# Reordering the input stage of a two-layer decoder kernel: x ahead of the tables, two bias products in two column groups

## The chip, the cores and the metric

The kernel runs on one NeuronCore of one Trainium2 chip, in one launch. The metric is the device time of that core in microseconds (us). Before the change the median of three runs is 1153.02 us (1152.75 to 1153.35). Engines are named as the profile names them: PE (TensorE), PEld (its weight loads), DVE (VectorE), ACT (ScalarE), POOL (GpSimd), SP (SyncE); SPq and ACTq are the issuing of DMAs on SP and on ACT.

## The reference: what is computed

A decoder trunk of two layers on x of 512 tokens by 1024 channels, all in float32. Layer 0 has sparse attention with an indexer that picks 128 keys per query, layer 1 sliding-window attention with sinks; each is followed by a SwiGLU block.

```python
for layer in range(DEPTH):
    h = rms_norm(x, attn_norm[layer])
    if layer % N_MIXERS == 0:
        x = x + dsa_mixer(h, a_w_in[j], a_latent_norm[j], a_w_uv[j], a_w_out[j], rel_bias)
    else:
        x = x + swa_mixer(h, b_w_in[j], b_b_in[j], b_sinks[j], b_w_out[j], b_b_out[j], rel_bias)
    h = rms_norm(x, ffn_norm[layer])
    x = x + swiglu(h, ffn_w_gate_up[layer], ffn_w_down[layer])
return rms_norm(x, final_norm)
```

Both mixers add a bias to their logits, `rel_bias[rel_bucket(distance)]`, from one table of 32 buckets by 16 heads. The part of the kernel that the change touches is what stands ahead of the first projection `h @ a_w_in`: x has to be loaded and turned so that channels lie on partitions, the norm gains have to be turned, and the bias table is spread out over distances.

## The kernel before

The order of the work is written out by hand, one program for each engine, with semaphores between them. x is held turned, as eight blocks (m = 0 to 7) of 128 channels by 512 tokens. Nearly all matrix products are done three times over in a rounded type (`mm3`, lines 613 to 615): high weights by high x, high weights by low x, low weights by high x. Weights come from memory as slabs of 128 x 2048 in `raw`. For each half of a slab (128 x 1024) ACT writes the rounded part `w_hi` (line 1162), then POOL writes the rest `w_lo` (line 501), then PE may use it (`lo_done`).

The input stage, which is the first 15 us or so, goes as follows.

- SP issues, in this order, the identity `tab` (L401), the 59 rows of norm gains and biases `par_rows` (L402), the first half of the channels of x for token blocks 0 and 2 (L395), half of the first weights (L399), the second half of x for these blocks, the rest of the first weights, the masks `tab_a` (L408) and the second slab (L410). It then waits for `g_sb` and stores it as `bias_row` (L414). Of `x_tok`, each DMA moves 128 tokens by 512 channels, 256 KB.
- ACT issues the one-hot table `hot` (33 rows of 4 KB, L1198), `rel_sb` (the bias table, L1199), and both halves of x for token blocks 1 and 3 (L1203). "fore" is the first half of the channels (all four DMAs add to the semaphore `x_in_fore`), "rear" the second.
- PE turns `par_rows` (L677), and multiplies `rel_sb` by the two halves of `hot` in two products of 512 columns (L681 into bank 6 and L684 into bank 7, both on output partitions 0 to 15, the second behind a wait for `par_done`). Then it turns x with 32 transposes of 128 x 128 (L671), 16 for the fore half and 16 for the rear half. Then it begins the first projection (L613 to L615).
- DVE copies the turned gains to `params` (L1603), the two products to `g_sb` (L1608, L1609), and for each block of x it makes `xs_lo` (L1614) and the copy `x` (L1618).
- ACT makes `xs_hi` for each block (L1211). Behind blocks 1 and 5 it casts a half of the first weights slab (L1162); POOL follows with `w_lo` (L501).

The first projection product waits for `lo_done` of the first half slab, for `xlo_done` of block 0, and for two blocks of `x`. Being in order on PE, it also stands behind all 32 transposes.

Of the kernel before, what the change touches and what calls it, by code (L numbers as in the profile page):

```python
# [7 lines left out]
F32 = mybir.dt.float32  # L8
# [6 lines left out]
T = 512  # L15
# [4 lines left out]
H = 16  # L20
# [4 lines left out]
BUCKETS, MAX_DIST = 32, 128  # L25
# [15 lines left out]
C_ID, C_DUP, C_CAUSAL, C_HOT = 0, P, 2 * P, 3 * P  # L41
ROW_A, ROW_B = 640, 384
GLEN = ROW_A + ROW_B
C_END = C_HOT + GLEN

S_A1, S_A2, S_AO, S_F0, S_D0 = 0, 3, 11, 15, 37
S_BK, S_BQ, S_BO, S_F1, S_D1, S_END = 53, 54, 58, 62, 84, 100
# [30 lines left out]
def tables():  # L78

    t = np.zeros((P, C_END), np.float32)  # L80
    i = np.arange(P)
# [13 lines left out]
def trunk(nc, x_in, rel_bias, par_in, a_w_in, a_w_uv, a_w_out, b_w_in, b_sinks, b_w_out,  # L95
          w_gate_up, w_down, consts, bias_row, bias_toep, out):
    ctx = ExitStack()
    with ctx:
        def sb(name, shape, dt=F32, where=ctx):
            return where.enter_context(nc.sbuf_tensor(name, shape, dt))  # L100

        def sem(name):
            return ctx.enter_context(nc.semaphore(name))
# [44 lines left out]
        early = ExitStack()  # L148
        x_tok = sb("x_tok", [P, NB, D], F32, early)
        hot = sb("hot", [BUCKETS + 1, GLEN], F32, early)  # L150
        g_sb = sb("g_sb", [H, GLEN], F32, early)
        rel_sb = sb("rel_sb", [BUCKETS + 1, H], F32, early)
        par_rows = sb("par_rows", [59, P], F32, early)
        early.close()
# [77 lines left out]
        ps = ctx.enter_context(nc.psum_tensor("ps", [P, 8, T], F32))  # L232
# [16 lines left out]
        hot_in = sem("hot_in")  # L249
# [10 lines left out]
        g_mm, g_done, row_out, toep_out = sem("g_mm"), sem("g_done"), sem("row_out"), sem("toep_out")  # L260
# [58 lines left out]
        def _(sp):  # L319
            def slab(n, it, src):  # L320

                for dst, s in src(n % 2):
                    if n == S_BK + 2:

                        sp.wait_ge(lo_done, 2 * (S_BK - 1))
                    elif n >= 2:

                        sp.wait_ge(lo_done, 2 * (n - 1) + 4 * it)
                    sp.dma_start(dst, s).then_inc(raw_full[n % 2], 16)

            def wide(w, c0):

                def src(slot):
                    v = raw[:, slot, :].rearrange("p (k n) -> p k n", k=DM)
                    g = w.rearrange("(k p) n -> p k n", p=P)
                    return [(v[:, 4 * i:4 * i + 4, :], g[:, 4 * i:4 * i + 4, bass.ds(c0, 256)])
                            for i in range(2)]
                return src
# [52 lines left out]
            def x_part(half):  # L391

                c = slice(half * T, (half + 1) * T)
                for t in (0, 2):
                    sp.dma_start(x_tok[:, t, c], x_in[0, t * P:(t + 1) * P, c]).then_inc(x_in_s[half], 16)  # L395

            def latent_part(k, n, done):

                sp.dma_start(r0[:, k:k + n, :], aw[:, k:k + n, A_CKV:A_CKV + 2 * P]).then_inc(done, 16)  # L399

            sp.dma_start(tab[:, 0:P], consts[:, 0:P]).then_inc(id_in, 16)  # L401
            sp.dma_start(par_rows[:, :], par_in).then_inc(small_in, 16)  # L402
            x_part(0)
            latent_part(0, 4, raw_fore)
            x_part(1)
            for k in (4, 6):
# [4 lines left out]
                    .then_inc(raw_full[1], 16)  # L411

            sp.wait_ge(g_done, 2)
            sp.dma_start(bias_row, g_sb[:, :]).then_inc(row_out, 16)  # L414
            slab(2, 0, wide(a_w_in[0], A_QI + P))
            sp.dma_start(sink[:, :], b_sinks[0:1, :].broadcast_to([P, H])).then_inc(sink_in, 16)
            sp.dma_start(uv_raw[:, :, :], a_w_uv[0].rearrange("h r c -> r h c")).then_inc(uv_full, 16)
            sp.wait_ge(row_out, 16)
            for n in range(S_A2, S_AO):
                slab(n, 0, wide(a_w_in[0], (n - S_A2) * 256))  # L420
                if n < S_A2 + 4:
# [75 lines left out]
        def _(pool):  # L497
# [29 lines left out]
            def q_part(h):  # L527

                if h == 0:

                    pool.wait_ge(row_out, 16)

                pool.wait_ge(qh_done, h + 1)
                nc.gpsimd.tensor_tensor(q_lo[:, h, :], q_new[h % 2], q_hi[:, h, :].bitcast(F32),
                                        ALU.subtract).then_inc(ql_done, 1)

            split_lo(S_A2 + 2)
            for h in range(3):
                q_part(h)
# [6 lines left out]
            for h in range(3, 7):  # L546
                q_part(h)
            for i in range(3, 6):
                split_lo(S_A2 + 2 + i)
                q_part(2 * i + 1)  # L550
                q_part(2 * i + 2)
# [58 lines left out]
        def _(pe):  # L610
# [52 lines left out]
            def x_turn(half):  # L663

                pe.wait_ge(x_in_s[half], 16 * NB)
                for m in range(half * DM // 2, (half + 1) * DM // 2):
                    if m == 6:

                        pe.wait_ge(g_done, 2)
                    for t in range(NB):  # L670
                        last = nc.tensor.transpose(ps[:, m, t * P:(t + 1) * P],  # L671
                                                   x_tok[:, t, m * P:(m + 1) * P], ident)
                    last.then_inc(x_tr, 1)
# [4 lines left out]
            pe.wait_ge(hot_in, 32)  # L678
            pe.wait_ge(rel_one, 1)

            nc.tensor.matmul(ps[0:H, 6, :], rel_sb[:, :], hot[:, 0:T], start=True, stop=True).then_inc(g_mm, 1)  # L681

            pe.wait_ge(par_done, 1)
            nc.tensor.matmul(ps[0:H, 7, 0:GLEN - T], rel_sb[:, :], hot[:, T:GLEN], start=True, stop=True).then_inc(g_mm, 1)  # L684
            x_turn(0)
            x_turn(1)

            pe.wait_ge(x_new, 2)
# [13 lines left out]
            for i in range(1, NB):  # L702
                last = nc.tensor.transpose(ps[:, 7, i * JI:(i + 1) * JI], kw[DH:DH + JI, i * P:(i + 1) * P],
                                           ident[DH:DH + JI, DH:DH + JI])
# [297 lines left out]
            for s in range(NB):  # L1002
                last = nc.tensor.transpose(ps[:, 7, s * P:(s + 1) * P], kv[:, 1, s * P:(s + 1) * P], ident)
# [139 lines left out]
        def _(act):  # L1143
# [41 lines left out]
            def xs_hi_m(m):  # L1185
                return xs_hi[:, bass.ds(m * T, T)]
# [8 lines left out]

                nc.scalar.activation(spare[:, 0:1], eps[:, :], func)

            act.dma_start(hot[:, :], consts[0:BUCKETS + 1, C_HOT:C_END]).then_inc(hot_in, 16)  # L1198
            act.dma_start(rel_sb[0:BUCKETS, :], rel_bias).then_inc(hot_in, 16)  # L1199
            for half in range(2):  # L1200
                c = slice(half * T, (half + 1) * T)
                for t in (1, 3):
                    act.dma_start(x_tok[:, t, c], x_in[0, t * P:(t + 1) * P, c]).then_inc(x_in_s[half], 16)  # L1203

            act.wait_ge(set_up, 4)
            load_table(ACT.Sqrt)
# [2 lines left out]
            for m in range(DM):  # L1209
                act.wait_ge(x_tr, m + 1)  # L1210
                nc.scalar.activation(xs_hi_m(m), ps[:, m, :], ACT.Copy,  # L1211
                                     scale=params[:, GAIN[0] + m:GAIN[0] + m + 1]).then_inc(xhi_done, 1)
                if m in (1, 5):
                    split_half(0, m // 4)
            split_hi(1)
            for m in range(DM):
# [351 lines left out]
        def _(dve):  # L1568
# [20 lines left out]
            def norm(e):  # L1589
# [14 lines left out]
            dve.wait_ge(par_done, 1)  # L1604
            nc.vector.tensor_scalar(nq_bias[:, :], params[:, B_IN:B_IN + DM], -float(DH) ** -0.5, None, ALU.mult)\
                .then_inc(nqb_done, 1)
            dve.wait_ge(g_mm, 2)
            nc.vector.tensor_copy(g_sb[:, 0:T], ps[0:H, 6, :]).then_inc(g_done, 1)  # L1608
            nc.vector.tensor_copy(g_sb[:, T:GLEN], ps[0:H, 7, 0:GLEN - T]).then_inc(g_done, 1)  # L1609

            for m in range(DM):

# [383 lines left out]
```

## Time and profile before

| | |
|---|---|
| median of 3 runs | 1153.02 us (1152.75 to 1153.35) |
| the profiled execution: its own time | 1152.82 us |
| its span, from first to last instruction | 1151.0 us |
| PE busy | 1135.0 us, 99% |
| DVE, ACT, POOL busy | 43%, 39%, 51% |
| PE first busy at | 5.38 us |
| first projection product (L613) starts at | 15.34 us |

The profile is of one execution, with times from the start of the span. A group of instructions is told as line, engine, operation, the tile written and the tiles read. Matmuls are pipelined, so that the duration of one is longer than the distance to the next: of 512 columns in the rounded type one takes 0.39 us and the next begins 0.23 us later. A float32 product shows as two instructions (x2). For a DMA the profile gives the time from issue to landing, where it could be found. The chain of waits is followed back from the last instruction.

### The profile page before, as it was taken

What the parts mean: (1) busy time and instruction counts of PE and PEld (TensorE: products, weight loads), DVE (VectorE), ACT (ScalarE), POOL (GpSimd) and SP (SyncE); (2) the same over time, 40 slices, a digit from 0 to 9 for tenths busy, and PEclk for the clock granted to TensorE, in tenths of its full rate; (3) what the DMA queues carried; (4) which work ended last, traced back from release to release, by engine and by line L of the source; (5) the groups of instructions that cost most, each with busy time, mean ns of one, the idle gap of its engine ahead of it and who ended that gap; (6) DMA issues with size and microseconds to landing.
All of it is one profiled execution on the core that took longest, in us unless ns stands there. A gap on an engine that the chain in (4) does not pass through costs nothing.

```text
span 1151.0 us, 15730 instructions
## 1 busy us (share of the span) xinstructions
PE 1135.0 (99%) x5538; PEld 928.1 (81%) x5538; DVE 496.7 (43%) x873; ACT 444.5 (39%) x829; POOL 590.7 (51%) x325
## 2 busy tenths in 40 slices
PE   8999999999999999999999999999999999999997
PEld 6778888778888888888888887788888888888887
DVE  6489956623534444441111366455443443420001
ACT  5353267743432322322222477544233233232333
POOL 4427767844544545434444487654454454444441
PEclk9999999999999999999999999999999999999999
DMA  7442311223233332324433333123323323223231
GB/s 240 160 138 73 129 37 56 74 74 109 75 109 89 93 109 80 102 80 123 147 111 108 98 98 78 38 84 99 110 73 109 102 81 109 84 78 98 79 100 73
DMA packets 180531, 112.45 MB, mean 98 GB/s; under 512 B 6300, under 2 KB 174551, under 8 KB 180488
## 3 DMA queue, kind: packets, MB, share of 16 engines
q1 hardware_dynamic: 179820, 110.71, 32.2%
q10 hardware_dynamic: 668, 1.19, 0.3%
q8 instruction: 24, 0.39, 0.1%
q14 instruction: 19, 0.16, 0.0%
HBM read 109.72 MB, written 8.45 MB: 103 GB/s over the span
## 4 chain that ended last, share of the span: by engine, by line
PE 93%; DVE 2%; POOL 2%; issue 1%; ACT 1%; DMA 0%; ACTq 0%; DVEq 0%; SPq 0%
PE ps L613 28%; PE ps L615 28%; PE ps L614 28%; PE ps L871 1%; PE ps L851 1%; DVE work L1691 1%; PE ps L622 1%; PE ps L1062 1%; POOL b_prob L596 1%; PE ps L822 1%; POOL w_lo L501 1%; PE ps L1036 1%; PE ps L671 1%; DVE work L1673 0%; DMA par_rows<-in_parameter_rows 0%
## 5 line engine op out<-in xcount | busy, mean ns | idle before, releaser
L501 POOL TENSOR_TENSOR w_lo<-raw,w_hi 128x1024 fp32r<-128x1024 f32 (+1 forms) x198 | 454.3, 2318 | 478.0 <-ACT w_hi L1162 469.6
L613 PE MATMUL ps<-xs_hi,w_hi 128*128 128x512 f32 x960 | 377.2, 393 | 1.1 <-DVE q_odd L1655 0.6
L614 PE MATMUL ps<-xs_lo,w_hi 128*128 128x512 f32 x960 | 373.7, 389 | 0.0
L615 PE MATMUL ps<-xs_hi,w_lo 128*128 128x512 f32 x960 | 373.6, 389 | 0.0
L1162 ACT CAST w_hi<-raw 128x1024 fp32r<-128x1024 f32 (+1 forms) x194 | 177.1, 963 | 434.8 <-PE ps L615 434.8
L613 PEld LDWEIGHTS ps<-xs_hi,w_hi 128*128 128x128 f32 x960 | 180.2, 188 | 41.9 <-issue 2.2
L614 PEld LDWEIGHTS ps<-xs_lo,w_hi 128*128 128x128 f32 x960 | 180.2, 188 | 37.7 <-issue 1.0
L615 PEld LDWEIGHTS ps<-xs_hi,w_lo 128*128 128x128 f32 x960 | 180.2, 188 | 37.8
L613 PE MATMUL ps<-act_hi,w_hi 128*128 128x512 f32 (+1 forms) x374 | 141.6, 378 | 0.0
L615 PE MATMUL ps<-act_hi,w_lo 128*128 128x512 f32 (+1 forms) x374 | 140.9, 377 | 0.0
L614 PE MATMUL ps<-act_lo,w_hi 128*128 128x512 f32 (+1 forms) x374 | 140.8, 377 | 0.0
L1813 DVE TENSOR_TENSOR glu<-std,up 128x512 f32<-128x512 f32 x44 | 67.8, 1540 | 77.0 <-ACT std L1365 76.8
L1816 DVE TENSOR_TENSOR act_lo<-glu,act_hi 128x512 f32 (+1 forms) x44 | 74.9, 1703 | 42.8 <-ACT act_hi L1370 42.8
L1809 DVE TENSOR_TENSOR up<-ps,rstd 128x512 f32<-128x512 f32 x44 | 30.4, 691 | 138.6 <-PE ps L615 138.6
L1828 DVE TENSOR_TENSOR x<-ps,x 128x512 f32 (+1 forms) x15 | 10.4, 692 | 173.7 <-PE ps L615 173.7
L614 PEld LDWEIGHTS ps<-act_lo,w_hi 128*128 128x128 f32 x374 | 70.4, 188 | 12.8
L615 PEld LDWEIGHTS ps<-act_hi,w_lo 128*128 128x128 f32 x374 | 70.4, 188 | 12.8
L613 PEld LDWEIGHTS ps<-act_hi,w_hi 128*128 128x128 f32 x374 | 70.4, 188 | 12.7
L1370 ACT CAST act_hi<-glu 128x512 f32 (+1 forms) x44 | 27.3, 622 | 76.9 <-DVE glu L1813 76.9
L596 POOL TENSOR_SCALAR b_prob<-b_prob,b_rinv 128x256 f32<-128x256 f32 x48 | 46.1, 977 | 11.8 <-DVE b_rinv L1885 11.8
L1578 DVE SCALAR_TENSOR_TENSOR xs_lo<-x,params,xs_hi (+1 forms) x24 | 25.5, 1063 | 51.6 <-ACT xs_hi L1177 51.6
L561 POOL TENSOR_SCALAR prob<-prob,rinv 128x512 f32<-128x512 f32 (+2 forms) x24 | 29.5, 1246 | 16.6 <-DVE rinv L1758 16.6
(186 smaller groups left out, 1255.6 us busy)
## 6 DMA issues: line engine op xcount, KB each, us to landing
raw<-in_ffn_w_gate_up SPq DMA_DIRECT2D x88, 512.0 KB, 4.5
raw<-in_ffn_w_down SPq DMA_DIRECT2D x32, 384.0 KB, 3.4
raw<-in_ffn_w_down SPq DMA_DIRECT2D x32, 320.0 KB, 3.9
raw<-in_a_w_in SPq DMA_DIRECT2D x19, 512.0 KB, 5.1
bias_toep<-bias_row SPq DMA_DIRECT2D x4, 1024.0 KB
toep<-bias_toep SPq DMA_DIRECT2D x16, 256.0 KB, 2.6
raw<-in_a_w_out SPq DMA_DIRECT2D x8, 512.0 KB, 4.3
raw<-in_b_w_in SPq DMA_DIRECT2D x8, 512.0 KB, 4.9
```

Source lines behind the costliest of these rows:

```text
L501: nc.gpsimd.tensor_tensor(pieces(w_lo, n)[half], pieces(raw, n)[half], pieces(w_hi, n)[half].bitcast(F32), ALU.subtract)\
L561: nc.gpsimd.tensor_scalar(at, at, rinv[:, par, i:i + 1], None, ALU.mult).then_inc(nrm_done, 1)
L596: nc.gpsimd.tensor_scalar(at, at, b_rinv[:, k % 3, a, i:i + 1], None, ALU.mult)\
L613: nc.tensor.matmul(dst, wh, xh, start=start, stop=False, **kw)
L614: nc.tensor.matmul(dst, wh, xl, start=False, stop=False, **kw)
L615: return nc.tensor.matmul(dst, wl, xh, start=False, stop=stop, **kw)
L1162: nc.scalar.copy(pieces(w_hi, n)[half], pieces(raw, n)[half]).then_inc(hi_done, 1)
L1370: nc.scalar.copy(act_hi[:, j + 2 * it, :], glu[:, j % 2, :]).then_inc(ah_done, 1)
L1578: nc.vector.scalar_tensor_tensor(xs_lo[:, bass.ds(m * T, T)], x[:, m, :], params[:, bass.ds(gain + m, 1)], xs_hi[:, bass.ds(m * T, T)].bit ...
L1809: nc.vector.tensor_tensor(up[:, :], ps[:, b + 1, :], rstd[:, :], ALU.mult).then_inc(up_done, 1)
L1813: nc.vector.tensor_tensor(glu[:, v, :], silu[:, :], up[:, :], ALU.mult).then_inc(glu_done, 1)
L1816: nc.vector.tensor_tensor(act_lo[:, v + 2 * it, :], glu[:, v, :], act_hi[:, v + 2 * it, :].bitcast(F32), ALU.subtract)\
```

## The change

Four edits, all in the input stage.

1. On SP, the fore half of x (blocks 0 and 2) is issued ahead of `tab` and `par_rows`.
2. On ACT, the fore half of x (blocks 1 and 3) is issued ahead of `hot` and `rel_sb`, the rear half behind them.
3. The two bias products write the same PSUM bank 6, the first on partitions 0 to 15, the second on partitions 32 to 47 (`G_REAR` = 32), one right behind the other without the wait for `par_done` between them, which moves behind the turning of the fore half. `g_sb` takes the same form, 48 partitions by 512. DVE waits once for both products, and `bias_row` is stored by two DMAs of 32 KB in place of one of 64 KB.
4. ACT casts the first half slab of weights behind the first block of x and no longer behind the second.

```diff
-        g_sb = sb("g_sb", [H, GLEN], F32, early)
+        g_sb = sb("g_sb", [G_REAR + H, T], F32, early)
...
+            x_part(0)
             sp.dma_start(tab[:, 0:P], consts[:, 0:P]).then_inc(id_in, 16)
             sp.dma_start(par_rows[:, :], par_in).then_inc(small_in, 16)
-            x_part(0)
             latent_part(0, 4, raw_fore)
...
             sp.wait_ge(g_done, 2)
-            sp.dma_start(bias_row, g_sb[:, :]).then_inc(row_out, 16)
+            for at, c in ((0, 0), (G_REAR, T)):
+                sp.dma_start(bias_row[:, c:c + T], g_sb[at:at + H, :]).then_inc(row_out, 16)
...
-            nc.tensor.matmul(ps[0:H, 6, :], rel_sb[:, :], hot[:, 0:T], start=True, stop=True).then_inc(g_mm, 1)
+            for at, c in ((0, 0), (G_REAR, T)):
+                last = nc.tensor.matmul(ps[at:at + H, 6, :], rel_sb[:, :], hot[:, c:c + T], start=True, stop=True)
+            last.then_inc(g_mm, 1)
+            x_turn(0)
 
             pe.wait_ge(par_done, 1)
-            nc.tensor.matmul(ps[0:H, 7, 0:GLEN - T], rel_sb[:, :], hot[:, T:GLEN], start=True, stop=True).then_inc(g_mm, 1)
-            x_turn(0)
             x_turn(1)
...
+            x_part(0)
+            act.dma_start(hot[:, :], consts[0:BUCKETS + 1, C_HOT:C_END]).then_inc(hot_in, 16)
+            act.dma_start(rel_sb[0:BUCKETS, :], rel_bias).then_inc(hot_in, 16)
+            x_part(1)
...
-                if m in (1, 5):
+                if m in (0, 5):
                     split_half(0, m // 4)
...
-            dve.wait_ge(g_mm, 2)
-            nc.vector.tensor_copy(g_sb[:, 0:T], ps[0:H, 6, :]).then_inc(g_done, 1)
-            nc.vector.tensor_copy(g_sb[:, T:GLEN], ps[0:H, 7, 0:GLEN - T]).then_inc(g_done, 1)
+            dve.wait_ge(g_mm, 1)
+            for at in (0, G_REAR):
+                nc.vector.tensor_copy(g_sb[at:at + H, :], ps[at:at + H, 6, :]).then_inc(g_done, 1)
```

The queue of SP, from the program's start, before (line numbers of each are its own):

```order
L401 DMA tab<-in_tables 128x128
L402 DMA par_rows<-in_parameter_rows 59x128
L395 DMA x_tok<-in_x 128x512 x2
L399 DMA raw<-in_a_w_in 128x4x256
L395 DMA x_tok<-in_x 128x512 x2
```

The same place on SP after the change:

```order
L397 DMA x_tok<-in_x 128x512 x2
L404 DMA tab<-in_tables 128x128
L405 DMA par_rows<-in_parameter_rows 59x128
L401 DMA raw<-in_a_w_in 128x4x256
L397 DMA x_tok<-in_x 128x512 x2
```

`par_rows` moves from the second place on the queue to the fourth, behind 512 KB of x and the 64 KB of `tab`.

ACT from the program's start, its DMAs and its first work on x (`xs_hi`) and on the weights (`w_hi`), before:

```order
L1198 DMA hot<-in_tables 33x1024
L1199 DMA rel_sb<-in_rel_bias 32x16
L1203 DMA x_tok<-in_x 128x512 x4
L1196 ACT_TABLE_LOAD
L1196 ACTIVATE spare<-eps 128x1 [waits set_up]
L1211 ACTIVATE xs_hi<-ps,params 128x512 [waits x_tr,par_done]
L1211 ACTIVATE xs_hi<-ps,params 128x512 [waits x_tr]
L1162 CAST w_hi<-raw 128x1024 [waits raw_fore]
L1211 ACTIVATE xs_hi<-ps,params 128x512 [waits x_tr] x4
```

And after:

```order
L1206 DMA x_tok<-in_x 128x512 x2
L1209 DMA hot<-in_tables 33x1024
L1210 DMA rel_sb<-in_rel_bias 32x16
L1206 DMA x_tok<-in_x 128x512 x2
L1200 ACT_TABLE_LOAD
L1200 ACTIVATE spare<-eps 128x1 [waits set_up]
L1219 ACTIVATE xs_hi<-ps,params 128x512 [waits x_tr,par_done]
L1166 CAST w_hi<-raw 128x1024 [waits raw_fore]
L1219 ACTIVATE xs_hi<-ps,params 128x512 [waits x_tr] x5
```

Two of the x DMAs move ahead of the tables, and the cast of the first weights stands one `xs_hi` earlier.

PE from the program's start up to the first projection product, before:

```order
L677 MATMUL ps<-tab,par_rows 128x59 [waits small_in,id_in]
L681 MATMUL ps<-hot,rel_sb 16x512 [waits rel_one,hot_in]
L684 MATMUL ps<-hot,rel_sb 16x512 [waits par_done]
L671 MATMUL ps<-tab,x_tok 128x128 [waits x_in_fore]
L671 MATMUL ps<-tab,x_tok 128x128 x15
L671 MATMUL ps<-tab,x_tok 128x128 [waits x_in_rear]
```

And after:

```order
L680 MATMUL ps<-tab,par_rows 128x59 [waits small_in,id_in]
L685 MATMUL ps<-hot,rel_sb 16x512 [waits rel_one,hot_in]
L685 MATMUL ps<-hot,rel_sb 16x512
L674 MATMUL ps<-tab,x_tok 128x128 [waits x_in_fore]
L674 MATMUL ps<-tab,x_tok 128x128 x15
L674 MATMUL ps<-tab,x_tok 128x128 [waits x_in_rear,par_done]
```

The order of PE's work is the same as before: the turning of `par_rows`, which waits for `par_rows` and `tab`, still stands ahead of all the rest. Only the wait for `par_done` moved.

## Rows read from the trace of the kernel before

**Rows 1.** Page: busy time, share and instructions; the chain that ended last.
```profile
PE 1135.0 (99%) x5538; PEld 928.1 (81%) x5538; DVE 496.7 (43%) x873; ACT 444.5 (39%) x829; POOL 590.7 (51%) x325
...
PE 93%; DVE 2%; POOL 2%; issue 1%; ACT 1%; DMA 0%; ACTq 0%; DVEq 0%; SPq 0%
```

**Rows 2.** Chain of waits, 0 to 16 us: start, us, what.
```profile
0.73 0.40 SPq L401
...
1.19 4.05 DMA par_rows<-in_parameter_rows
...
5.38 0.33 PE ps L677
5.71 1.81 PE ps L681 x2
7.52 1.71 PE ps L684 x2
9.23 5.91 PE ps L671 x32
...
15.34 0.47 PE ps L613
```

**Rows 3.** Timeline of 0 to 16 us: start, us, engine, line, xcount, idle and releaser.
```profile
1.56 0.83 SPq L395 DMA_DIRECT2D x_tok<-in_x  x2
...
2.90 1.39 SPq L395 DMA_DIRECT2D x_tok<-in_x  x2
...
5.64 1.88 PE L681 MATMUL ps<-hot,rel_sb 33*16 33x512 f32 x2
...
9.16 5.98 PE L671 MATMUL ps<-tab,x_tok 128*128 128x128 f32 x32
...
10.37 1.48 ACT L1211 ACTIVATE xs_hi<-ps,params 128x512 fp32r<-128x512 f32 x2 [4.90 <-PE ps L671]
...
11.75 1.04 ACT L1162 CAST w_hi<-raw 128x1024 fp32r<-128x1024 f32 x1
...
12.87 2.37 POOL L501 TENSOR_TENSOR w_lo<-raw,w_hi 128x1024 fp32r<-128x1024 f32 x1 [9.92 <-ACT w_hi L1162]
```

**Rows 4.** DMA issues near 0.7 and near 2.9 us: size, us to landing.
```profile
tab<-in_tables SPq DMA_DIRECT2D x1, 64.0 KB, 2.8
...
x_tok<-in_x SPq DMA_DIRECT2D x1, 256.0 KB, 7.4
```

**Rows 5.** Windows: stretch, busy us of each engine, clock, DMA share, GB/s.
```profile
1.00:2.00 1.00, 0.00 (x0) 0.00 (x0) 0.03 (x1) 0.00 (x0) 1.00 (x3) 1.00 0.29 46
3.00:5.00 2.00, 0.00 (x0) 0.00 (x0) 0.00 (x0) 1.02 (x1) 0.00 (x0) 1.00 0.78 147
8.00:10.00 2.00, 2.00 (x6) 0.84 (x5) 0.73 (x2) 0.00 (x0) 0.00 (x0) 1.00 1.07 398
```

**Rows 6.** DMA queues in 8 to 9 us (q1 SP, q10 ACT): packets, share.
```profile
q10 hardware_dynamic: 140, 0.25, 66.2%
q1 hardware_dynamic: 139, 0.14, 40.4%
```

**Rows 7.** DMA packets in 4.3 to 4.5 us.
```profile
DMA packets 12, 0.01 MB, mean 61 GB/s; under 512 B 0, under 2 KB 8, under 8 KB 12
```

**Rows 8.** Timeline of PE near 52 us: products on two row groups.
```profile
52.31 0.28 PE L622 MATMUL ps<-q_hi,q_lo 64*128 64x256 f32 x2
52.43 0.28 PE L622 MATMUL ps<-q_hi 64*128 64x256 f32 x2
```

**Rows 9.** Lines L681 and L661: ns min/median/max of one float32 product of 512 columns.
```profile
L681 PE MATMUL ps<-hot,rel_sb x2: 1031/1044/1057, 5.6 to 6.5; 33*16 33x512 f32 x2
...
L661 PE MATMUL ps<-ss,ones x2: 590/590/591, 31.7 to 32.2; 128*128 128x512 f32 x2
```

**Rows 10.** Windows of L671 alone: stretch, PE busy, PEld busy (weight loads), clock.
```profile
9.10:12.60 3.50, 3.44 (x16) 3.28 (x17) 1.00 1.07 392
...
13.70:15.20 1.50, 1.44 (x13) 1.20 (x11) 1.00 1.01 335
```

More of the change, by code:

```diff
@@ L44 @@
 C_END = C_HOT + GLEN
+G_REAR = 32
 S_A1, S_A2, S_AO, S_F0, S_D0 = 0, 3, 11, 15, 37
@@ L417, in _ @@
             sp.dma_start(uv_raw[:, :, :], a_w_uv[0].rearrange("h r c -> r h c")).then_inc(uv_full, 16)
-            sp.wait_ge(row_out, 16)
+            sp.wait_ge(row_out, 32)
             for n in range(S_A2, S_AO):
@@ L529, in q_part @@
                 if h == 0:
-                    pool.wait_ge(row_out, 16)
+                    pool.wait_ge(row_out, 32)
                 pool.wait_ge(qh_done, h + 1)
@@ L1196, in load_table, with x_part @@
                 nc.scalar.activation(spare[:, 0:1], eps[:, :], func)
-            act.dma_start(hot[:, :], consts[0:BUCKETS + 1, C_HOT:C_END]).then_inc(hot_in, 16)
-            act.dma_start(rel_sb[0:BUCKETS, :], rel_bias).then_inc(hot_in, 16)
-            for half in range(2):
+            def x_part(half):
                 c = slice(half * T, (half + 1) * T)
```

## The prediction

> **What bounds the kernel now.** I read the page first: PE is busy for 1135.0 of 1151.0 us and carries 93% of the chain that ended last [rows 1]. So a change ahead of the first projection moves the end by as much as it moves the start of that projection, and by nothing else, unless a later stage is anchored to something other than PE. None is: the other engines wait there for PE, or PE for them after work that PE itself released. The question is when L613 starts, now 15.34 us.
>
> The chain of waits answers it for the first 16 us [rows 2]. From the bottom up: L613 stands behind 5.91 us of transposes (32 of L671), these behind 3.52 us of bias products (L681 and L684), these behind the turning of the gains (0.33 us), and this behind the DMA of `par_rows`, issued at 1.19 and landed at 5.24. No x is in the chain. The transposes began in the instant in which PE came free, so the fore half of x, issued from 1.56 on [rows 3], had landed by 9.16. So the two things that set the stage are when the 59 small rows land, and how long PE's own work behind them is.
>
> Beside it runs a second chain that is nearly as late [rows 3]: two `xs_hi` on ACT from 10.37, the cast of the first half slab 11.75 to 12.79, `w_lo` on POOL 12.87 to 15.24. L613 needs it, and PE's transposes ended at 9.23 + 5.91 = 15.14 [rows 2], so the two are level to 0.1 us.
>
> **The change part by part.** I count from two moments: L, when `par_rows` lands (now 5.24), and T, when the transposes begin (now 9.16).
>
> *From L to T.* PE begins 0.14 after the landing (5.38 less 1.19 + 4.05, rows 2), its first bias product 0.40 after it (5.64 less 5.24, rows 3). The two float32 products are four instructions; from 5.64 to 9.16 they take 3.52, thus 0.85 each with 0.1 over [rows 3, 9]. Nothing in this trace runs two column groups of the array at once. Two row groups do run side by side: the pairs of L622 near 52 us are counted as x2 in the time of one, 0.12 us from one pair to the next for 256 columns [rows 8]. But there the code issues one instruction for each group in turn. Here each product is itself two instructions for the same group, issued one behind the other, and PE starts its matmuls in order: A1, then A2 with B1 beside it, then B2. That is three times 0.85, 2.56 + 0.1 = 2.67 and not 1.8. The bounds are 1.8 (all in pairs) and 3.52 (nothing overlaps). I take the middle one, 2.67: a saving of 0.85. So T = L + 0.40 + 2.67 = L + 3.07.
>
> The Trainium skill (TensorE: Matmul & The Clock Gate, "Part 3: Packing small matmuls") says that tiles in different column groups overlap almost fully, 2.38 times faster with three of them, and that matmuls keep strict order; by the first half alone T would be L + 2.2, by the second it is the staggered case that I take. The rows on L622 agree with the order, and no row here shows columns.
>
> *L itself.* `par_rows` is now the fourth DMA of SP's queue. SP's issues are some 0.42 apart (two in 0.83, rows 3; 0.40 for `tab`, rows 2), so it is issued at about 0.73 + 3 x 0.42 = 2.0 and not at 1.19. If its 4.05 us stayed, it would land at 6.05: the lower bound. It will not stay. 29.5 KB took 4.05 us where the 64 KB of `tab`, issued 0.46 earlier, took 2.8 [rows 2, 4]. In 4.3 to 4.5 us the trace has 8 packets under 2 KB, thus one each 0.025 us [rows 7], the pace of a single DMA engine working through them one behind another; 59 such take 1.5 us. That engine now has to do first what stands ahead of it on SP's queue, and, since the two queues alternate packet by packet (139 and 140 packets in one microsecond, rows 6), also what ACT's queue holds. ACT's holds x fore, `hot` and x rear, all issued by about 3.5. Per engine, at one sixteenth of the rows: 16 packets of 2 KB from SP's x fore, 16 from ACT's x fore, 16 from ACT's x rear, 3 of 4 KB from `hot`, 8 small ones of `tab` and the 59. A 2 KB packet takes 0.662 x 16 / 140 = 0.076 us [rows 6], so 48 x 0.076 + 3 x 0.15 + 67 x 0.025 = 3.65 + 0.45 + 1.68 = 5.8 us. The first bytes flow about 1 us after the first issue (46 GB/s in 1 to 2 us, rows 5), at 1.7; thus 7.5, and some 0.3 for the last write and its semaphore: 7.8. To this comes the slow start that the trace has: 3 to 5 us moved 294 KB (147 GB/s) where the steady 398 GB/s would have moved 796 [rows 5], 1.3 us lost. With all of it L = 9.1. From the other side, a DMA of x rear that SP issued at 2.9 took 7.4 [rows 4]; the same latency from 2.0 gives 9.4, the upper bound. I take L = 8.6, in the upper half of 7.8 to 9.1, since x in front meets the slow start as it did before. So `par_rows` lands 3.4 us later than now.
>
> That one engine carries it is what the Trainium skill says too (DMA: Bandwidth & Descriptors, "Why a DMA increments its semaphore by 16 and not by 1"): a DMA uses the largest number of engines up to 16 that divides its rows, and 59 has no divisor but itself, thus one. By that rule, putting 512 KB ahead of it costs this transfer most of all, and the trace agrees with it by the 4.05 us against 2.8. If all 16 engines shared it instead, the sum would end near L = 6.5.
>
> *From T to L613.* T = 8.6 + 3.07 = 11.7, against 9.16: 2.5 later. Now the 32 transposes run through in 5.98 us without a gap for x rear [rows 3], whose DMAs keep their place; x fore is sooner. So nothing else stops the transposes. The cast of the first weights comes one `xs_hi` earlier. It starts when the first `xs_hi` ends: now 10.37 + 0.69 = 11.06, 1.90 after T, against 11.75, 2.59 after T. So `w_lo` ends 3.49 behind the start of the cast (15.24 less 11.75), at T + 5.4 in place of T + 6.08. The weights it needs were in by 11.75 [rows 3], and they keep their place on the queue; the cast will want them at 13.6, so that wait costs nothing. What remains last is PE itself: 32 transposes, of which the last weight load begins at T + 5.7 and L613 could start at T + 5.82. The gain of this edit is thus only what `w_lo` was late by, 15.34 less 14.98 = 0.36. Sum: 11.7 + 5.8 = 17.5 us, 2.15 later than 15.34.
>
> One term in this can move: the transposes get faster midway. 16 of them take 3.44 us in 9.1 to 12.6 (0.215 each), but 11 weight loads go by in 1.2 us from 13.7 on (0.109 each) [rows 10], and a float32 product of 512 columns takes 1.04 at 5.6 us and 0.59 at 31.7 [rows 9]. The page's grant reads 1.00 throughout, yet these durations show the lower of the clock's two levels, 1.2 GHz, up to 13.7 and 2.4 GHz from there, 4.5 us after the transposes began. If the rise comes at the same 13.7 whatever PE does, only 9 of the 32 are slow and `w_lo` is last, at T + 5.4 + 0.1: 17.2. If it comes only after all of them, 32 x 0.213 = 6.8: 18.5. With the rise as far behind T as now, 17.5.
>
> *The rest.* DVE's two copies of `g_sb` (0.68 each, DVE idle there) still lie beside the transposes and ahead of the first `xs_hi`. `bias_row` goes out as two DMAs; the next thing on SP's queue is a slab that waits for POOL at 18.5 anyway. Cost nothing. `w_lo` of later halves is 2 us and more ahead of PE and moves with it. Tables and x rear have slack.
>
> The middle of 17.2 and 17.5, less 15.34, is 1.9 to 2.1 us; I take +1.9. The profiled execution took 1152.82, 0.2 under the median of the runs, so the same shift is put on the median: 1153.0 + 1.9 = 1154.9.
>
> **The rivals.**
>
> *The reordering works as it reads.* `par_rows` is held up only by its later issue (L = 6.05 to 6.9), and the two products overlap fully. Then T = 6.05 + 0.40 + 1.8 = 8.25, L613 at 14.1, 1.3 us sooner: 1151.8; with L = 6.9 it is 1152.6. For it: x fore lands sooner, at about 6, and the DMA engines moved only 147 GB/s in 3 to 5 us [rows 5]. Against it: the packets alternate and one engine does the 59. It decides for faster once L is under 5.24 + 1.7 = 6.9 with full overlap, or under 6.1 + 0.36 with the stagger. This is the faster side: chance 0.13, none of it faster by over 0.2%.
>
> *The small rows land very late and the clock rises late.* L = 9.4, products in series (3.52), the transposes all at 1.2 GHz: T = 13.3, L613 at 19.1 to 20.1, thus +3.8 to +4.8: 1157 to 1158. For it: the 7.4 us of the DMA of x rear, and that no row shows column groups overlapping. A milder form, with just one of the three (L = 9.4, or series, or the late rise), gives +2.7 to +3.0: 1155.8 to 1156.0. Chance of either form: 0.30.
>
> *The start stage is hidden anyway*: a later stage waits for something older than PE, and the shift is absorbed there. PE's waits later on are for POOL and ACT work released by PE; nothing speaks for it. 1153.0, chance 0.05.
>
> **How the numbers follow.** The forecast, +0.3 to +2.6 us (L from 7.6 to 8.9 with the stagger), has 0.52. A measurement of this kernel tells 0.2%, 2.3 us, from no change. Faster by more than that: nothing here reaches it, 0.03 for what I don't see. Slower by more: of the forecast's 0.52 a fifth lies over +2.3, 0.10, and of the late rival 0.28, thus 0.38. Within 0.2%: the rest, 0.59. The range: down to 1152.0, which takes in most of the first rival, and up to 1156.8, which takes in the mild form of the second; 0.15 to 0.2 lie outside.
>
> **What would show it.** In the profile after: the chain of waits again begins with the DMA of `par_rows`, landing between 7.8 and 9.4 (right) or under 7 (the first rival). The bias products span 2.7 us from the first start to the first transpose (stagger), 1.8 (full) or 3.5 (series). x fore lands sooner than now and waits for PE. The cast runs right behind the first `xs_hi`, without a wait for `raw_fore`. L613 starts near 17.4, and from there to the end the two profiles are the same length to 0.5 us. The prediction is wrong in its core if `par_rows` lands before 7 us, or if the shift at L613 isn't the shift at the end.

## The result and the profile after

| | before | after |
|---|---|---|
| median | 1153.03 us | 1155.43 us |
| range of 16 runs each | 1152.67 to 1154.34 | 1155.11 to 1156.65 |
| profiled execution, its span | 1152.82, 1151.0 | 1155.27, 1153.5 |
| `par_rows` landed | 5.24 | 10.09 |
| transposes of x begin (T) | 9.16 | 12.30 |
| first projection product | 15.34 (L613) | 17.77 (L616) |

The change makes the kernel 2.4 us slower: ratio 1.0021, 95% interval 1.0014 to 1.0028. The forecast was 1154.9, a shift of 1.9; the measured shift is 2.4.

The page after, first the busy times, then the engines' shares of the chain that ended last:

```profile
PE 1132.9 (98%) x5538; PEld 927.7 (80%) x5538; DVE 496.5 (43%) x873; ACT 444.1 (38%) x829; POOL 590.1 (51%) x325
...
PE 93%; DVE 2%; POOL 2%; issue 1%; ACT 1%; DMA 1%; SPq 0%; ACTq 0%; DVEq 0%
```

Beside [rows 1], PE does as many instructions and is busy 2.1 us less in a span 2.5 us longer; the chain's share by DMA goes from 0% to 1%. So something at a DMA grew. The chain of waits after, 0 to 18.3 us (start, us, what), says which:

```profile
2.12 7.97 DMA par_rows<-in_parameter_rows
...
10.23 0.33 PE ps L680
10.55 1.82 PE ps L685 x4
12.37 5.64 PE ps L674 x32
18.01 0.23 PE ps L616
```

Against [rows 2]: the same links in the same order. The DMA of `par_rows` begins 0.93 later and takes 7.97 us in place of 4.05; the products take 1.82 in place of 3.52; the transposes 5.64 in place of 5.91. The rest of the stage, in the timeline after (columns as in [rows 3]):

```profile
10.48 1.89 PE L685 MATMUL ps<-hot,rel_sb 33*16 33x512 f32 x4
12.30 5.71 PE L674 MATMUL ps<-tab,x_tok 128*128 128x128 f32 x32
...
13.52 0.69 ACT L1219 ACTIVATE xs_hi<-ps,params 128x512 fp32r<-128x512 f32 x1 [8.38 <-PE ps L674]
14.11 1.04 ACT L1166 CAST w_hi<-raw 128x1024 fp32r<-128x1024 f32 x1
...
15.22 2.37 POOL L504 TENSOR_TENSOR w_lo<-raw,w_hi 128x1024 fp32r<-128x1024 f32 x1 [12.28 <-ACT w_hi L1166]
...
17.77 0.48 PE L616 MATMUL ps<-xs_hi,w_hi 128*128 128x512 f32 x1
```

The cast follows the first `xs_hi` without a wait. `w_lo` ends at 17.59, and PE begins at 17.77. The DMAs after, of those issued from about 1.2 to 2.2 us (size, us to landing), and the windows as in [rows 5]:

```profile
x_tok<-in_x ACTq DMA_DIRECT2D x1, 256.0 KB, 4.5
x_tok<-in_x SPq DMA_DIRECT2D x1, 256.0 KB, 5.1
...
tab<-in_tables SPq DMA_DIRECT2D x1, 64.0 KB, 5.5
```
```profile
1.00:2.00 1.00, 0.00 (x0) 0.00 (x0) 0.02 (x1) 0.00 (x0) 1.00 (x3) 1.00 0.33 25
2.00:4.00 2.00, 0.00 (x0) 0.00 (x0) 0.00 (x0) 0.35 (x1) 0.94 (x1) 1.00 0.89 214
3.00:5.00 2.00, 0.00 (x0) 0.00 (x0) 0.00 (x0) 1.34 (x2) 0.00 (x0) 1.00 0.92 308
```

x fore is complete at about 6.3 (SP's last issue at about 1.18, plus 5.1) and waits six microseconds for PE. `tab`, issued at 1.64, lands at 7.1; the 59 small rows behind it need three more. The trace's packet records show how: the rows, packets of 512 bytes, go one at a time from 6.25 to 9.34 us. Most follow each other after some 0.025 us, but between 6.9 and 8.9 there are 16 steps of 0.12 us on average, and right behind nearly every such row there begins a 2 KB packet of ACT's queue, which takes 0.08 to 0.1 us. That is how one engine that alternates between two queues would look. The semaphore follows at 10.09, 0.75 behind the last row.

### The profile page after: what moved, and what is told of

It reads as the page before. It is cut to its first block, busy times and chain, and to the rows that moved or that the text cites. A ratio compares the mean times of both kernels' runs of the same rounds, so it can differ in the third digit from the quotient of the medians.

```text
span 1153.5 us, 15732 instructions
## 1 busy us (share of the span) xinstructions
PE 1132.9 (98%) x5538; PEld 927.7 (80%) x5538; DVE 496.5 (43%) x873; ACT 444.1 (38%) x829; POOL 590.1 (51%) x325
## 4 chain that ended last, share of the span: by engine, by line
PE 93%; DVE 2%; POOL 2%; issue 1%; ACT 1%; DMA 1%; SPq 0%; ACTq 0%; DVEq 0%
PE ps L616 28%; PE ps L617 28%; PE ps L618 28%; PE ps L875 1%; PE ps L855 1%; DVE work L1699 1%; PE ps L625 1%; PE ps L1066 1%; POOL b_prob L599 1%; PE ps L826 1%; DMA par_rows<-in_parameter_rows 1%; POOL w_lo L504 1%; PE ps L1040 1%; PE ps L674 0%; DVE work L1681 0%
## 5 line engine op out<-in xcount | busy, mean ns | idle before, releaser
L616 PE MATMUL ps<-xs_hi,w_hi 128*128 128x512 f32 x960 | 377.2, 393 | 0.9 <-DVE q_odd L1663 0.6
L616 PEld LDWEIGHTS ps<-xs_hi,w_hi 128*128 128x128 f32 x960 | 180.2, 188 | 41.8 <-issue 2.2
L616 PE MATMUL ps<-act_hi,w_hi 128*128 128x512 f32 (+1 forms) x374 | 141.6, 378 | 0.0
L616 PEld LDWEIGHTS ps<-act_hi,w_hi 128*128 128x128 f32 x374 | 70.4, 188 | 12.6
```

Of the source, the lines that this page charges most:

```text
L616: nc.tensor.matmul(dst, wh, xh, start=start, stop=False, **kw)
```

## The experiments

Each kernel is after or before with the edit shown. "First product" is the start of the first projection product in the profiled execution; the last column is what of the span lies behind it.

| kernel | built on | median us (n) | ratio to before, 95% | first product | span less it |
|---|---|---|---|---|---|
| before | | 1153.03 (16) | | 15.34 | 1135.7 |
| after | | 1155.43 (16) | 1.0014 to 1.0028 | 17.77 | 1135.7 |
| a2_rows_split | after | 1153.06 (11) | 0.9991 to 1.0009 | 16.11 | 1135.7 |
| a1_rows_first | after | 1153.78 (11) | 0.9995 to 1.0013 | 17.14 | 1135.8 |
| a6_first_and_split | after | 1153.51 (11) | 0.9990 to 1.0008 | 15.68 | 1137.3 |
| a5_same_columns | after | 1156.95 (6) | 1.0020 to 1.0044 | 19.44 | 1135.8 |
| b1_sp_order | before | 1156.92 (6) | 1.0020 to 1.0044 | 17.65 | 1135.8 |
| b2_act_order | before | 1156.17 (9) | 1.0017 to 1.0036 | 18.62 | 1135.8 |
| b3_pair_alone | before | 1153.10 (11) | 0.9990 to 1.0008 | 15.89 | 1135.7 |
| b4_cast_alone | before | 1152.95 (11) | 0.9989 to 1.0007 | 15.17 | 1135.7 |
| c0_split_alone | before | 1152.86 (11) | 0.9989 to 1.0007 | 14.76 | 1137.3 |
| c1_combined | before | 1153.09 (11) | 0.9996 to 1.0014 | 15.18 | 1135.7 |
| d1_turn_x_first | after | 1153.97 (11) | 0.9996 to 1.0015 | 16.22 | 1138.2 |
| e1_turn_x_first_cast_second | after | 1152.46 (11) | 0.9989 to 1.0007 | 15.26 | 1135.7 |

The medians of before that ran beside them lay at 1153.03 to 1153.09. A profile is of one execution, and five lie off their median: a1 (1154.64), a6 (1154.81), c0 (1153.86) and d1 (1156.18) above it, b1 (1155.18) below it, so the start of the first product is not that of a typical execution there. Eleven of the fourteen profiles have the same 1135.7 to 1135.8 us behind the first product, whatever was done ahead of it; the three others are taken up at the end.

**Is it the transfer of the rows?** `a2_rows_split`: the 59 rows as 48 and 11, in the same place of the queue.

```diff
-            sp.dma_start(par_rows[:, :], par_in).then_inc(small_in, 16)
+            for r0_, r1_ in ((0, 48), (48, 59)):
+                sp.dma_start(par_rows[r0_:r1_, :], par_in[r0_:r1_, :]).then_inc(small_in, 16)
```

> The changed kernel with par_rows loaded by two DMAs, of 48 and of 11 rows, in the same place on SP's queue, behind x and tab. Theory E (the DMA of 59 rows is worked off by one DMA engine, packet by packet against ACT's x): the rows spread over engines and land 0.3 to 0.6 us behind tab (7.1 us in the changed kernel), near 7.7; products start near 8.0, transposes near 9.8, the first projection product near 15.2: 1152.9. Rival Q2 (what counts is the place on the queue alone, the number of rows does not matter): it still lands near 10 us and the time stays at 1155.4.

Measured 1153.06 (1152.80 to 1154.38). Its chain of waits:

```profile
2.59 5.00 DMA par_rows<-in_parameter_rows
...
7.72 0.33 PE ps L681
8.05 1.82 PE ps L686 x4
9.87 6.49 PE ps L675 x32
```

The rows land at 7.59, 2.5 us sooner, though the second of the two DMAs is issued 0.47 later than the one before; the time falls by 2.4, the whole loss. In the packet records all rows are through by 6.41, where the 59 ended at 9.34. The transfer was slow by its row count, not by its bytes or place alone. The place still costs: the rows land 2.35 us later than in before, and it is the shorter products that pay for most of this. The first product came 0.9 later than expected, because the transposes took 6.49 us.

`a1_rows_first`: the other way to relieve it, SP's old order with the rest of the change.

```diff
-            x_part(0)
             sp.dma_start(tab[:, 0:P], consts[:, 0:P]).then_inc(id_in, 16)
             sp.dma_start(par_rows[:, :], par_in).then_inc(small_in, 16)
+            x_part(0)
```

> The changed kernel with SP's queue in the old order (tab and par_rows ahead of x); ACT's queue, the paired products and the early cast stay. Theory Q (par_rows waits behind x on its own queue): it lands near 5.3 us in place of 10.1. Then hot is last, which stands behind two x DMAs on ACT and landed near 7.7 us in the changed kernel: the products start at 7.7 to 8.0, the transposes at 9.7, the first projection product (L613 of before) near 15.2: 2.5 us under the changed kernel, 1152.9. Rival A (the DMA engines are simply full of x, whichever queue it stands on): par_rows still lands after 8 us and the time stays above 1154.5.

Measured 1153.78 (1153.00 to 1154.64; the profile is of the last of these). Its chain has a new head, the other thing that PE's first work wants:

```profile
2.32 6.75 DMA rel_sb<-in_rel_bias
...
9.11 1.89 PE ps L685 x4
11.00 6.38 PE ps L674 x32
```

Both theories missed the rows: PE turns them at 7.78, so that they landed near 7.64, neither at 5.3 nor after 8. First on SP's own queue, they are still held up by the x that now stands first on ACT's:

```profile
7.78 0.33 PE L680 MATMUL ps<-tab,par_rows 59*128 59x59 f32 x1 [7.78 <-DMA par_rows<-in_parameter_rows]
```

With SP repaired, edit 2 is the bound: `hot` and `rel_sb` stand behind ACT's x fore, and `rel_sb` lands last, at 9.07. `a6_first_and_split` adds the split of `par_rows` (the diff of a2) to a1:

> The run with tab and par_rows first on SP, x first on ACT, now with par_rows as 48 and 11 rows. If it was the one engine with all 59 rows that held hot back to 9.07 us there (it too had its share of hot), hot and rel_sb now land near 7.4 us, par_rows near 4.4; products 7.5 to 9.3, transposes from 9.3, first projection product at 15.1 to 15.8: 1152.7 (1152.4 to 1153.4). If hot was late for another reason it stays near 9 us and the time at 1153.8.

Measured 1153.51 (1152.26 to 1154.81), just over the expected range. The rows are in at 5.0, and PE waits for the same two tables, till 8.31 and not 7.4. Behind the products x fore, which follows the rows on SP, is as late as they are. Timeline, then chain:

```profile
8.35 1.89 PE L686 MATMUL ps<-hot,rel_sb 33*16 33x512 f32 x4 [2.89 <-DMA rel_sb<-in_rel_bias]
```
```profile
2.50 7.74 DMA x_tok<-in_x
```

**What is each edit worth alone?** `b1_sp_order` is before with edit 1 (the reverse of a1's diff), `b2_act_order` before with edit 2:

```diff
-            act.dma_start(hot[:, :], consts[0:BUCKETS + 1, C_HOT:C_END]).then_inc(hot_in, 16)
-            act.dma_start(rel_sb[0:BUCKETS, :], rel_bias).then_inc(hot_in, 16)
             for half in range(2):
...
+                if half == 0:
+                    act.dma_start(hot[:, :], ...)
+                    act.dma_start(rel_sb[0:BUCKETS, :], rel_bias)
```

> The kernel before with only SP's queue changed (x's fore half for blocks 0 and 2 ahead of tab and par_rows). Theory E (one DMA engine works off par_rows, behind its share of x from both queues and against ACT's rear half): it lands near 10.1 us as in the changed kernel, the two products in series end 3.9 us later, the transposes start near 14.0 and the first projection product near 19.4: 1156.8 to 1157.1. Rival (both queues must be changed for the harm): par_rows lands under 8 us, time under 1155.

> The kernel before with only ACT's queue changed (x's fore half for blocks 1 and 3 ahead of hot and rel_sb). par_rows and hot land as in the run with the rows first, near 7.6 and 9.0 us, since x now stands ahead of hot and the single engine of par_rows alternates with x; the products, in series, run 9.1 to 12.7 and the first projection product starts near 18: 1155.5 (1154.8 to 1156.2). Rival (ACT's order is harmless, only SP's costs): 1153.1.

Measured: b1 1156.92 (1155.18 to 1157.81), +3.9; b2 1156.17 (1155.86 to 1156.84), +3.1. Their chains, b1 (whose profile is of its fastest run, 1155.18), then b2:

```profile
2.12 5.45 DMA par_rows<-in_parameter_rows
...
7.70 0.33 PE ps L677
8.03 1.81 PE ps L681 x2
9.84 1.71 PE ps L684 x2
```
```profile
2.32 6.55 DMA rel_sb<-in_rel_bias
...
8.92 1.89 PE ps L681 x2
10.81 1.71 PE ps L684 x2
12.51 6.10 PE ps L671 x32
```

In b1's profiled execution the rows land at 7.56 and not near 10.1, which is what the rival said. Only 512 KB of x stand ahead there and are in at 5.1; ahead of the 59 rows is a gap of 0.7 us, as long as eight of ACT's 2 KB packets, and then they run from 5.65 to 7.19, one each 0.026 us, with no room for other packets between them. So the engine does not always alternate one by one, and why it did in after and not here is open. PE waits 1.2 us more, for DVE's `x`, before its first product. The other five executions took 1156.55 to 1157.81, about what the late landing would give; no profile shows their rows.

By the medians each reordering alone loses over 3 us. They overlap, since PE waits only for the later of the two arrivals, and their sum is not what the whole costs.

`b3_pair_alone` is before with edit 3 (that part of the change's diff):

```diff
-            nc.tensor.matmul(ps[0:H, 6, :], rel_sb[:, :], hot[:, 0:T], ...).then_inc(g_mm, 1)
+            for at, c in ((0, 0), (G_REAR, T)):
+                last = nc.tensor.matmul(ps[at:at + H, 6, :], rel_sb[:, :], hot[:, c:c + T], ...)
```

> The kernel before with only the two products side by side (and g_sb, bias_row that go with them). The products end at 7.4 us in place of 9.2 and x's fore half, which landed by then, is turned from 7.5 us on. If PE were all that bounds the stage the first projection product would start at 13.6 (1151.3). I expect less: it needs w_lo, which follows the cast, which needs the first weights, landed near 11.2 us. Cast at 11.3, w_lo ends at 14.75, the first projection product starts near 14.9: 0.45 us sooner than before, 1152.6. Rival (the weights do not bind): 1151.3.

Measured 1153.10 (1152.83 to 1153.58), no change, where 1152.6 was expected. The timeline says where 1.7 us of shorter products went:

```profile
5.40 1.89 PE L685 MATMUL ps<-hot,rel_sb 33*16 33x512 f32 x4
...
9.36 3.67 PE L674 MATMUL ps<-tab,x_tok 128*128 128x128 f32 x16 [2.07 <-DMA x_tok<-in_x]
...
13.34 2.79 PE L674 MATMUL ps<-tab,x_tok 128*128 128x128 f32 x16 [0.30 <-DMA x_tok<-in_x]
```

PE is free at 7.3 and x fore is not there until 9.3; the rear half is late again. In before, the products were the cover of x's transfer, nearly to the microsecond.

`b4_cast_alone` is before with edit 4:

```diff
-                if m in (1, 5):
+                if m in (0, 5):
```

> The kernel before with only the cast of the first half slab moved ahead of the second xs_hi. The cast can start no sooner than the first weights have landed, 11.2 us, against 11.75 before; w_lo ends at 14.7, and PE's transposes (last load near 14.9) are then last: first projection product at 15.0, 0.3 us sooner, 1152.7. Rival (the cast in front delays the later xs_hi blocks and with them PE): 1153.2 or more.

Measured 1152.95 (1152.46 to 1154.40), no change that can be told. The cast comes 0.34 us behind the end of the first `xs_hi` and not at once, since the weights are just in:

```profile
11.51 1.05 ACT L1162 CAST w_hi<-raw 128x1024 fp32r<-128x1024 f32 x1 [0.34 <-DMA raw<-in_a_w_in]
```

**Do the two products really run side by side?** `a5_same_columns` is after with both on partitions 0 to 15, in banks 6 and 7 (the gains are turned into bank 5):

```diff
-            for at, c in ((0, 0), (G_REAR, T)):
-                last = nc.tensor.matmul(ps[at:at + H, 6, :], rel_sb[:, :], hot[:, c:c + T], ...)
+            for at, c in ((0, 0), (0, T)):
+                last = nc.tensor.matmul(ps[at:at + H, 6 + (c > 0), :], rel_sb[:, :], hot[:, c:c + T], ...)
```

> The changed kernel with both bias products on output partitions 0 to 15, in banks 6 and 7 (the turned gains go to bank 5 for that); all else as changed. Theory: on one column group nothing overlaps, four instructions of 0.85 us take 3.5 us in place of 1.8, the transposes start 1.7 us later (14.0), the clock rises as far behind them or up to 1 us nearer, so 1156.4 to 1157.1. Rival (the gain came from dropping the wait for par_done between the two and not from the columns): 1.8 us stays, 1155.4.

Measured 1156.95 (1156.38 to 1157.33), 1.5 over after. Its chain has the same late rows and the old price of the products:

```profile
2.12 8.00 DMA par_rows<-in_parameter_rows
...
10.25 0.33 PE ps L680
10.58 3.52 PE ps L685 x4
```

The windows of the products alone (stretch, PE busy, PEld busy, clock, DMA share, GB/s), of after and then of a5, show how it comes about:

```profile
10.40:10.80 0.40, 0.32 (x2) 0.13 (x4) 1.00 1.06 379
10.80:11.30 0.50, 0.50 (x2) 0.00 (x0) 1.00 1.11 391
```
```profile
10.40:10.80 0.40, 0.29 (x1) 0.12 (x2) 1.00 1.08 387
```

In after, two matmuls are under way and four weight loads done within 0.4 us; with the same columns it is one and two. The first halves of both products start together. Edit 3 works fully, and is worth 1.5 of the 1.7 us here, because in after there is no x to wait for.

**Is there a version that gains?** `c0_split_alone` is before with the rows as 48 and 11 (a2's diff).

> The kernel before with par_rows loaded as 48 and 11 rows, nothing else. Theory E: the one engine that held all 59 rows finishes 1.2 to 1.5 us sooner, so all transfers behind it land sooner too: par_rows near 4.3, x fore 7.1 to 7.8 in place of 8.6 to 9.3, x rear near 11.3 in place of 12.6. PE starts about 0.8 us sooner; the series of products ends at 8.3, so the transposes start at 8.3; then w_lo is last (first weights at about 10, cast at 10.9): first projection product near 14.5, 1152.2 (1152.0 to 1152.6). Rival Q2 (the number of engines does not matter): 1153.1.

Measured 1152.86 (1152.22 to 1154.51), which can't be told from before and is above the expected range. The rows land at 4.3 and the first product is 0.58 sooner, but x fore came at 8.4 and sets T (timeline):

```profile
8.46 3.67 PE L672 MATMUL ps<-tab,x_tok 128*128 128x128 f32 x16 [0.19 <-DMA x_tok<-in_x]
...
12.52 1.97 PE L672 MATMUL ps<-tab,x_tok 128*128 128x128 f32 x16 [0.39 <-DMA x_tok<-in_x]
```

`c1_combined` puts the split, the pair and the early cast on before, and shares the first weights between the two queues ahead of x rear:

```diff
-            latent_part(0, 4, raw_fore)
+            latent_part(0, 2, raw_fore)
...
+                if half == 0:
+                    act.dma_start(raw[:, 0, :]...[:, 2:4, :], a_w_in[0]...[:, 2:4, ...]).then_inc(raw_fore, 16)
```

> A version from the findings: the kernel before with par_rows as 48 and 11 rows, the paired products, the early cast, and the first half slab of weights split between SP's and ACT's queues ahead of x's rear half. Products 4.4 to 6.4 us, inside the wait for x; x fore lands at 7.3 to 7.8, first weights by 9.5, so the cast runs right behind the first xs_hi (9.6), w_lo ends at 13.1; PE's transposes, 5.8 to 6.5 us of them, are last: first projection product at 13.5 to 14.2, 1151.5 (1151.2 to 1152.0). Rival (x rear, now further back, is late and PE stalls between the two halves of the transposes): 1152.3 or more.

Measured 1153.09 (1152.38 to 1156.57), no gain, as the rival said. PE now waits twice for x, 3.5 us in all. That is about what it had saved: its products begin 1.0 us sooner and take 1.7 less, and the transposes 0.6 less (timeline):

```profile
8.68 3.46 PE L675 MATMUL ps<-tab,x_tok 128*128 128x128 f32 x16 [2.20 <-DMA x_tok<-in_x]
...
13.48 1.94 PE L675 MATMUL ps<-tab,x_tok 128*128 128x128 f32 x16 [1.34 <-DMA x_tok<-in_x]
```

`d1_turn_x_first` goes the other way: after's early x is used at once. `tab` is first on SP, the rows are split, and PE turns x block 0, then the gains, then blocks 1 to 3, and only then multiplies:

```diff
             pe.wait_ge(id_in, 16)
-            pe.wait_ge(small_in, 16)
+            x_turn(0, (0,))
+            pe.wait_ge(small_in, 32)
             nc.tensor.transpose(ps[:, 7, 0:59], par_rows[:, :], ident[0:59, 0:59]).then_inc(par_t, 1)
+            x_turn(0, (1, 2, 3))
```

> The changed kernel with tab first on SP, then x, par_rows as 48 and 11 rows, and on PE the turning of x's fore half ahead of the bias products (par_rows turned behind its first block; DVE copies g_sb behind block 1). x fore lands at 6.5 us and PE starts then and no longer waits for rows or hot; 0.33 + 1.8 of other work and 5.8 to 6.5 of transposes end at 14.5 to 15.2: first projection product at 14.7 to 15.3, 1152.5 (1152.2 to 1153.0). Rival (g_sb's copies, now late on DVE, hold PE before block 6, or x rear does): 1153.5 or more.

`e1_turn_x_first_cast_second` is d1 with the cast behind the second block again, as in before:

```diff
-                if m in (0, 5):
+                if m in (1, 5):
```

> The run that turns x first, with the cast of the first half slab back behind the second xs_hi. There the cast sat at the head of ACT for 0.85 us waiting for the weights, so the second xs_hi and DVE's copies of g_sb behind it came late and PE waited 1.5 us for them, long enough for the clock to fall back in 14.5 to 17.9 us. Now the second xs_hi runs while the weights are still on their way; g_sb is copied by 13.6, when PE reaches block 6 at 13.7, so PE no longer waits; w_lo ends near 13.8. First projection product at 14.0 to 15.0, 1152.2 (1151.7 to 1152.7) in runs in which the clock then stays up; a run in which it falls back once later (as three profiles had near 213 us) takes 1.7 us more. Rival (the DMAs bind: x rear lands after 12 us): 1153 or more, with a wait for x_tok in the middle of the transposes.

Measured: d1 1153.97 (1152.77 to 1156.18), e1 1152.46 (1151.61 to 1154.33). In the profiled execution of d1, its slowest, the early cast hurts, because the weights are not in and the cast holds up ACT's next `xs_hi` and so DVE's `g_sb`; in e1 it does not wait. Timelines of d1, then of e1:

```profile
10.23 1.04 ACT L1168 CAST w_hi<-raw 128x1024 fp32r<-128x1024 f32 x1 [0.85 <-DMA raw<-in_a_w_in]
...
14.60 1.97 PE L675 MATMUL ps<-tab,x_tok 128*128 128x128 f32 x8 [1.46 <-DVE g_sb L1621]
```
```profile
7.44 1.08 PE L675 MATMUL ps<-tab,x_tok 128*128 128x128 f32 x4 [7.44 <-DMA x_tok<-in_x]
...
14.42 1.09 PE L675 MATMUL ps<-tab,x_tok 128*128 128x128 f32 x8 [0.47 <-DVE g_sb L1621]
```

e1 has the lowest median and the lowest single run of all, 0.6 us under its own before and 3 under after, but the interval holds 1: against before it is not shown to be faster. Its first product, at 15.26, is later than the 14.0 to 15.0 expected. The expectation puts the fall of the clock in d1 down to PE's wait, but c1 waits 1.34 us too, and the 16 transposes behind it take 1.94 us, at the higher clock; the wait alone does not decide it. What e1 still waits for are the two banks (6 and 7) that the products and the gains share with the last blocks of x.

## Why the prediction was right, and where it erred

**The bound.** Right: what moved the first product moved the end by as much. The shift at the first product was +2.43 and that of the span +2.5, and the constant 1135.7 us behind it in eleven profiles shows it for every other edit too.

**L, when the rows land.** The mechanism was right, the size not: 10.09 against 8.6, and outside the upper bound of 9.4. One DMA engine carries the 59 rows behind its share of all that is ahead of it, and between part of them went ACT's packets, one by one; the packets of after show it, and a2 takes this away and the loss with it. By the Trainium skill (DMA: Bandwidth & Descriptors, "Why a DMA increments its semaphore by 16 and not by 1") 48 rows go on 16 engines and 11 on eleven; the 2.5 us agree. The 1.5 us by which L was short stand in three terms of the sum. What is ahead of the rows on their engine makes 32 x 0.076 + 0.45 + 8 x 0.025 = 3.1 us, and from the first bytes at 1.7 the rows would have begun at 4.8; they began at 6.25, thus 1.45 lost where the forecast had put 0.8, although it had counted 1.3. That x in front meets the slow start was right, but the start is not the same as before: 3 to 5 us moved 308 GB/s and not 147, and the loss had been made by then, in 1 to 4 us. The rows took 3.1 us, where 59 x 0.025 plus 16 packets of x between them, 16 x 0.076, make 2.7. And the last write and its semaphore took 0.75 and not 0.3. The upper bound failed because it was read from a DMA of 128 rows, which was not held up as the one of 59 was.

**The pair.** Wrong, in the favourable sense: 1.82 (12.30 less 10.48) and not 2.67. The step that failed is "PE starts its matmuls in order: A1, then A2 with B1 beside it, then B2". After's window shows the first halves of both starting together. Had each product run its two halves before the other began, there would be no such pair. Whether the engine passes over the waiting second half or the halves stand in the program in another order than the source has it, no run here tells. The half of the Trainium skill's statement that the forecast set aside (TensorE: Matmul & The Clock Gate, "Part 3: Packing small matmuls", different column groups overlap almost fully) is the one that the trace and a5 bear out.

**The tail.** Right. The cast starts at T + 1.81 (forecast 1.90), `w_lo` ends at T + 5.29 (5.4), the first product stands at T + 5.47 (5.4 to 5.8). It is `w_lo` and PE in a tie again, with the clock rise 4.1 us behind T and not 4.5.

**The sum.** L +1.5, the pair -0.85, the tail -0.35 make +0.3 at the first product (17.77 against 17.2 to 17.5); the sum went to +1.9 only by taking a value between, and the median moved by 2.4. Two errors of opposite sign made the forecast look better than its steps were; that they nearly cancelled is luck. The measured 1155.4 lies as near to the milder late rival (1155.8) as to the forecast (1154.9), so that the time alone would not have told them apart.

**The rest.** x fore sooner and waiting, `bias_row` in two DMAs and the copies of `g_sb` at no cost: right. The rival that the reordering works as it reads needed L under 6.9; it was 10.09. The late rival had the late rows right (past its 9.4), and the series and the late clock wrong. Not foreseen at all was how little there is to gain in the other direction: b3, c0 and c1 take 1.0 to 3.3 us of work or waiting from PE ahead of x, and their first products come 0.55 us later, 0.58 and 0.16 sooner, because x, over two queues that move some 390 GB/s, is only then complete.

## What to carry to other kernels

Before moving a small transfer back in a queue, look at its row count: with 59 rows one DMA engine did it all, behind its share of everything ahead; 48 + 11 cost one more issue and gave 2.5 us behind x, and about 1 us at the front of the queue, where the time did not show it. What an engine's first instruction waits for stays in front, or that instruction is changed, as in e1, to be one that wants what is in front (3 us better than after, not shown better than before). And a chain in which x does not stand can have x as its next bound: ask for each saved microsecond at what time the next operand lands.

## What the runs showed of the hardware

- Two float32 products of 512 columns and 33 rows take 1.82 us on two column groups and 3.52 on one, both at the lower clock.
- The DMA of 59 rows of 512 bytes went row by row: in 1.54 us where no other queue's packets came between (b1), in 3.1 us where for 16 of the rows a 2 KB packet of the other queue did (after).
- The clock can fall back far from any edit. In c0 the first product is 0.58 us sooner and the span 1.1 longer. The windows of c0 (columns as in [rows 5]) and the same stretches of before:

```profile
210.00:213.00 3.00, 1.40 (x11) 0.93 (x10) 1.47 (x5) 1.50 (x5) 3.00 (x4) 1.00 0.30 74
213.00:216.00 3.00, 3.00 (x16) 3.00 (x15) 1.26 (x6) 1.81 (x6) 2.99 (x3) 0.59 0.06 18
```
```profile
210.00:213.00 3.00, 1.40 (x8) 0.68 (x7) 1.72 (x6) 2.04 (x8) 3.00 (x4) 1.00 0.14 17
213.00:216.00 3.00, 3.00 (x22) 2.83 (x22) 1.86 (x8) 1.68 (x5) 3.00 (x3) 1.00 0.21 76
```

  PE is busy 1.40 of 3 us in both; in one the clock then falls (0.59 on average) and 16 matmuls fit where 22 did, in the other it stays. a6 shows the same, and d1 has two such falls; these are the three profiles with 1.6 to 2.5 us more behind the first product. It is not a property of the kernel alone: of c0's 11 executions the three slowest have a mean granted clock of 0.997, the others 0.998 or 0.999. A gain of half a microsecond drowns in it, and what decides between fall and no fall stays open.
- The rise of the clock is no fixed time behind the start of the transposes. The 32 of them took 6.49 us in a2, 5.64 in after and 5.01 in a6. This moves the first product by as much as many of the edits did.
